# Extra TensorE passes over the next weight chunk inside four layer norms

## The reference

```python
def layer_norm_2(x, g, b):
    xf = x.astype(jnp.float32)
    mu = jnp.mean(xf, -1, keepdims=True)
    var = jnp.mean(jnp.square(xf - mu), -1, keepdims=True)
    return ((xf - mu) * lax.rsqrt(var + NORM_EPS) * g.astype(jnp.float32) + b.astype(jnp.float32)).astype(x.dtype)

# first block: modulation, multiscale pooling as mixer, then
x = layer_norm(ALPHA * x + g1 * ox, ln_g[i, 0], ln_b[i, 0])                      # norm 0
x = layer_norm(ALPHA * x + g2 * swiglu(x * (1.0 + sc2) + sh2, ...), ...)         # norm 1
# second block: for each of two layers, the mixer m is latent attention, then a hyena convolution
x = layer_norm_2(DEEPNORM_ALPHA * x + m, ln1_g[i], ln1_b[i])                     # norms 2 and 4
x = layer_norm_2(DEEPNORM_ALPHA * x + conv_ffn(x, ...), ln2_g[i], ln2_b[i])      # norms 3 and 5
```

## Time and profile before

| | us |
|---|---|
| median of three runs | 2030.12 |
| lowest, highest | 2022.63, 2033.9 |
| profiled execution | 2031.26 |
| its span, first to last instruction | 2029.9 |
| mean granted clock of PE | 0.938 |

### The profile page before, as it was taken

One profiled execution on the slowest core, in us unless ns is written; L12 is line 12 of the kernel. 1 busy time (PEld: TensorE's weight loads), 2 busy tenths in 40 slices (PEclk: granted clock), 3 DMA queues, 4 the chain that ended last, 5 costly groups with the idle time before them and its releaser, 6 DMA issues.

```text
span 2029.9 us, 19622 instructions
## 1 busy us (share of the span) xinstructions
PE 1820.0 (90%) x7784; PEld 1446.5 (71%) x7784; DVE 998.3 (49%) x1393; ACT 626.5 (31%) x882; POOL 777.3 (38%) x360
## 2 busy tenths in 40 slices
PE   3687899999989989989999998998575989999997
PEld 1455788888867666768888786787465768888785
DVE  7885533330263846454444125424999464444224
ACT  1333322221233534243333223222222243333222
POOL 3543344444434020334444443443453324444442
PEclk9897999999989987979999998999788979999998
DMA  8662332232222010213233221431111312232222
GB/s 310 248 228 100 104 100 98 93 100 97 90 63 83 21 63 1 83 55 101 93 97 101 94 93 63 166 97 70 62 42 57 110 62 94 94 103 94 94 94 73
DMA packets 54340, 197.45 MB, mean 97 GB/s; under 512 B 6215, under 2 KB 6535, under 8 KB 52392
## 3 DMA queue, kind: packets, MB, share of 16 engines
q1 hardware_dynamic: 52584, 190.06, 28.0%
q10 hardware_dynamic: 1664, 6.13, 0.9%
HBM read 183.58 MB, written 12.58 MB: 97 GB/s over the span
## 4 chain that ended last, share of the span: by engine, by line
PE 77%; DVE 14%; ACT 3%; POOL 2%; DMA 2%; issue 2%; SPq 0%; ACTq 0%; DVEq 0%
PE ps L440 24%; PE ps L442 24%; PE ps L441 23%; POOL w_lo L1234 2%; PE ps L476 1%; DVE x_residual L1783 1%; PE ps L783 1%; DVE n_values L1504 1%; DVE mod_ring L1374 1%; DVE act_lo L1509 1%; ACT act_hi L1011 1%; DVE x_residual L1773 1%; ACT w_hi L905 1%; DVE x_residual L1775 1%; DVE hy_product_lo L1787 1%
## 5 line engine op out<-in xcount | busy, mean ns | idle before, releaser
L1234 POOL TENSOR_TENSOR w_lo<-w_raw,w_hi 128x1024 fp32r<-128x1024 f32 x258 | 622.0, 2411 | 993.5 <-ACT w_hi L905 993.5
L440 PE MATMUL ps<-act_hi,w_hi 128*128 128x512 f32 x1428 | 572.7, 401 | 43.8 <-DVE act_lo L1509 20.8
L442 PE MATMUL ps<-act_hi,w_lo 128*128 128x512 f32 x1428 | 565.5, 396 | 0.0
L441 PE MATMUL ps<-act_lo,w_hi 128*128 128x512 f32 x1428 | 565.4, 396 | 0.0
L905 ACT ACTIVATE w_hi<-w_raw 128x1024 fp32r<-128x1024 f32 x258 | 273.2, 1059 | 734.5 <-PE ps L442 729.3
L440 PEld LDWEIGHTS ps<-act_hi,w_hi 128*128 128x128 f32 x1428 | 274.0, 192 | 119.8 <-issue 26.1
L442 PEld LDWEIGHTS ps<-act_hi,w_lo 128*128 128x128 f32 x1428 | 273.9, 192 | 58.8
L441 PEld LDWEIGHTS ps<-act_lo,w_hi 128*128 128x128 f32 x1428 | 274.6, 192 | 56.0 <-issue 0.5
L440 PE MATMUL ps<-f_hidden_hi,w_hi 128*128 128x512 f32 x528 | 209.8, 397 | 1.7 <-POOL w_lo L1234 1.7
L442 PE MATMUL ps<-f_hidden_hi,w_lo 128*128 128x512 f32 x528 | 208.4, 395 | 0.0
L441 PE MATMUL ps<-f_hidden_lo,w_hi 128*128 128x512 f32 x528 | 208.4, 395 | 0.0
(11 more groups left out here) (250 smaller groups left out, 2299.8 us busy)
## 6 DMA issues: line engine op xcount, KB each, us to landing
w_raw<-in_w_stream SPq DMA_DIRECT2D x258, 512.0 KB, 3.7
mod_ring<-in_mod_t SPq DMA_DIRECT2D x26, 512.0 KB, 5.9
x_tokens<-in_mod_t SPq DMA_DIRECT2D x22, 512.0 KB, 6.1
spectra<-filter_spectra SPq DMA_DIRECT2D x16, 512.0 KB, 3.3
hy_filter<-spectra SPq DMA_DIRECT2D x8, 1024.0 KB, 4.7
x_residual<-in_xT ACTq DMA_DIRECT2D x8, 256.0 KB, 7.9
x_tokens<-in_x_tokens SPq DMA_DIRECT2D x1, 2048.0 KB, 8.1
x_spill<-x_residual SPq DMA_DIRECT2D x8, 256.0 KB, 9.9
```

Of the source, the lines that this page charges most:

```text
L440: PE.matmul(o, lh, rh, start=start, stop=False, **kw)
L441: PE.matmul(o, lh, rl, start=False, stop=False, **kw)
L442: return PE.matmul(o, ll, rh, start=False, stop=stop, **kw)
L1234: GP.tensor_tensor(B.WL[:, c % 2, :], B.WR[:, c % 2, :], f32(B.WH[:, c % 2, :]), ALU.subtract).then_inc(S.w_lo, 1)
```

## The change

`norm(i)` on PE gets three rows of extra matmuls, for i = 1 to 4. Each multiplies the first block of the chunk that the next stage begins with, 128x128, by the first 512 columns of that same chunk, and writes bank 2, which nobody reads before it is overwritten. Six stand ahead of the wait for y_sum, eight between the column sums and the inverse rows, ten behind the inverse rows. Ahead of the first six, PE waits for that chunk's w_lo and for the third output tile of the stage before to be added. Norm 5 is unchanged.

```diff
--- before.py
+++ after.py
@@ -601,13 +601,29 @@
         PE.wait_ge(S.x_sum, i)
         PE.matmul(ps[:, 6, :], B.lead_w[:, :], B.x_sum[:, :], start=True, stop=True).then_inc(S.ln_mean, 1)
 
+    def keep_busy(slot, n):
+
+        for _ in range(n):
+            PE.matmul(ps[:, 2, :], B.WH[:, slot, 0:P], B.WH[:, slot, 0:T], start=True, stop=True)
+
     def norm(i):
+        follows = AFTER_NORM[i]
+        if follows is not None:
+            slot = FIRST_CHUNK[follows] % 2
+            chunk(FIRST_CHUNK[follows])
+
+            PE.wait_ge(S.x_ready, 8 * i + 3)
+            keep_busy(slot, 6)
         PE.wait_ge(S.y_sum, i)
         PE.matmul(ps[:, 6, :], B.mean_w[:, :], B.x_sum[:, :], start=True, stop=True).then_inc(S.ln_shift, 1)
         columns(1, B.x_sum, True)
         PE.wait_ge(S.sq_added, 7 * i)
         columns(0, B.sq_sum, False).then_inc(S.ln_turned, 1)
+        if follows is not None:
+            keep_busy(slot, 8)
         inverse_rows_of(i, 3)
+        if follows is not None:
+            keep_busy(slot, 10)
 
     def out_linear(name, i, rh, rl):
```

## The result

Fourteen executions of each kernel: 2014.09 us in the median after the change (2005.49 to 2022.39), 2022.12 before (2016.8 to 2033.9). The ratio is 0.995, with a 95% interval of 0.9929 to 0.9972. So the change makes the kernel faster by about 0.5%: 8 us by the medians, 10 by the means.

A forecast was written before the change was run, and what follows sets the result against it. The kernel was taken as bound by PE nearly everywhere (77% of the chain). Terms 3.7 + 3.15 + 0.6 - 1.3 = 6.15 us, off the profiled 2031.26, gave 2025.1 us; 8-in-10 range 2017.5 to 2031.5.

The forecast's parts named there:

- The six passes: Ahead of the mean matmul: 1.4 us at full clock, inside waits of 1.51 to 2.06 us, so cost nothing.
- The eight: Between column sums and inverse rows: 1.95 us at full clock, costing 0.1 us a norm.
- Inverse rows: In each norm, 1.05 us at full clock instead of 2.08: 0.93 gained each after costs, 3.7 us in all.
- Column sums: Mean plus columns at full clock, 2.81 us, in norms 2 and 4 too: gain 3.15 us.
- The first scaling to w_hi: Thin stretch behind the inverse rows: clock still falls, 16.7 to 18.0 us; 0.6 us gained over four norms.
- the allowance of 1.3 us: Clock falls during the column sums in one norm in five, 1.6 us worse each: 1.3 us for four norms.
- Rival A: Ten passes hold the clock through the stretch behind the inverse rows: all 11.9 us gained, 2019.4 us; chance 0.17.
- the sum against 2031.26 us: Whole kernel: the 6.15 us gain taken off the profiled execution's 2031.26 us, giving 2025.1 us.
- rival C: Gain in the norms lost where the clock moves in attention and hyena stages; scatter about +-4 us, possibly 2030; chance 0.13.
- Rival B: Passes run at half clock where the path waits for them, in the norms: slower, 2036.9 us; chance 0.10.

The follow-up runs named there:

- eight16: The changed kernel with 16 instead of 8 passes ahead of the inverse rows; 2031.38 us, ratio 1.0023.
- norm1_only: The changed kernel with its passes in norm 1 alone, norms 2 to 4 as before; 2025.12 us, ratio 0.9984.
- fill: The changed kernel with six more passes in each of the three waits between the first four k-steps behind norms 1 to 4; 2010.91 us, ratio 0.9937.
- best2: The changed kernel plus passes in thin stretches, attention waits and norm 5, and eight ahead of the mean in norms 2 and 4; 2006.12 us, again 2010.18.
- after_again: The changed kernel unaltered, run again beside the kernel before; 2013.13 us, ratio 0.9954.
- after_third: The changed kernel unaltered, run a further time; 2012.17 us, ratio 0.9928.
- tiny: The changed kernel with each 512-column pass replaced by a one-column float32 matmul; 2021.2 us, ratio 0.9993.
- no_ten: The changed kernel without the ten passes behind the inverse rows; 2016.51 us, ratio 0.9951.

## Why the prediction was right and wrong

**The norms, term by term.** The six passes cost nothing: the mean starts 0.05 us behind x_sum. Right. The eight cost under 0.1 us: the rows start 1.77 to 1.81 us behind the columns, against 1.73 to 1.75. Right, and eight16 shows the price beyond that. Inverse rows: forecast 0.93 gained each, measured from columns to first scaling 2.94, 2.93, 2.93 and 2.94 us against 3.86, 3.85, 3.85 and 3.86: 3.7 us in all. Right. Column sums: 2.80 or 2.81 us in all four norms, 3.2 gained, right. The first scaling to w_hi: forecast 16.7 to 18.0, measured 17.6, 17.0, 17.4 and 16.8, a gain of 1.2 where 0.6 was said. Right, mechanism included: the clock fell 6.5 to 9 us behind the inverse rows and came back 12 to 14 us behind the first scaling, as the work piled up. (The bound of 18.0 is a little short: norm 1 of norm1_only took 18.21.) Rival A didn't come, save for one norm in twelve, though PE's idle gaps between the spread-out groups of norm 1 were no longer than 1.24 us; fill shows what it would have needed. The term of the norms that was mis-sized is the allowance of 1.3 us for a clock that falls in the column sums. It was not paid in any of the three profiles of the changed kernel. It is real: of the 40 norms in all profiles that have full passes on both sides of the column sums, 3 paid it, at 1.5 or 2.4 us (all three in fill and best2, whose code up to there differs from the changed kernel's in nothing that lies near; it looks like chance); one in five was too much. With that 1.3 and the 0.6 us more behind the first scaling, 8.1 us stand against 6.15.

**What it is added to.** The step that failed is the one that set the sum against 2031.26 us, with rival C's even scatter of +-4 us over it. The times don't scatter evenly. They lie in two clusters some 10 us apart, and the profiled execution before and two of the three runs shown belonged to the upper one, while 12 of the 14 executions after lie in the lower. Of the 11.0 us between 2025.1 and 2014.09, 9.1 are the distance from that execution to the median of fourteen before, and 1.9 are what the medians gained beyond 6.15. The trace had it in plain sight: 27 us at half clock with PE busy all the time, between 754 and 782, in a stage that the prediction left aside because the change doesn't touch it. The rule that the time is the profiled execution's less the gain holds only where both kernels' executions are of one cluster. Over all occasions the upper cluster's median is 2030.0 before and 2021.5 after, the lower one's 2018.4 and 2012.2: gains of 8.5 and 6.3 us. So there is luck in the 8 us by which the two medians of the result differ: on that occasion 6 of 14 executions before were in the upper cluster, elsewhere 60 of 88; where the changed kernel ran again (after_again, after_third), the medians before, 2027.9 and 2028.4, lie 14.8 and 16.2 us above its own. Rival C named the stage, and put a width on it instead of looking.

**The chances.** The ratio's interval crosses the line at 0.5%, so between faster and within nothing is decided by it. Rival B (the passes don't count, or come at half clock) was not seen in the changed kernel, and tiny shows what it would have taken.

## What to carry to other kernels

Passes of full width that lay wholly inside a wait kept PE's clock up for the work behind it; size them by the wait at full clock, because each one that overran a wait on the path was paid in full, and give them first to every short wait that stands ahead of dense work. In a long stretch that other engines pace, ten passes at its head bought nothing (no_ten); six more in each of its three gaps took another 0.8 us off that stretch in each norm (fill). Before a time is set against one profiled execution, read its clock over the whole span: a stretch at half clock in which PE is fully busy is an event that the next execution may not have. Here filling one wait of 2.2 us in each of the two attention groups, in a stage that the change doesn't touch, took away a whole cluster of slow executions.

## What the runs showed of the hardware

- PE 100% busy isn't enough to hold its clock: one-column matmuls with their weight loads let it fall from 1.0 to 0.5 (tiny), and 27 us of scores and transposes without a break didn't bring it back in the profile before, whereas the same work stayed at 1.0 when it started there (17.9 us against 30).
- The clock fell behind one and the same wait ahead of the scores (PE idle for 1.78 us) in some executions and not in others, 6 times in 20. Filled with seven passes it never showed the fall, in 12 + 11 + 6 + 6 executions without a time in the upper cluster.
- A pass of 512 columns over other data or into a bank that nobody reads costs DVE and ACT nothing: act_lo came at 2.29, 4.49, 6.69 and 8.89 us behind the first scaling with and without it.
